# Two weight loads of the expert layers wait until the routed rows are in memory

## The chip, the cores and the metric

The kernel runs on one core of one Trainium2 chip. Its time is the device time of one execution in microseconds (us). The engines of the core run side by side and meet at semaphores: TensorE (PE) multiplies, VectorE (DVE) and ScalarE (ACT) do element work, GpSimd (POOL) issues the indirect transfers here, and SyncE (SP) only issues DMA transfers, in the order of its program. ACT issues transfers too, on a DMA queue of its own. All queues of the core share the same 16 DMA engines.

## The reference

Two blocks of two layers each work on 512 tokens of width 1024, in float32. The first block holds both places that the change touches: after its forgetting attention (layer 0) and after its retention (layer 1) comes a mixture of 32 experts. A router picks two experts for each token, and each expert is a gated product:

```
hn = rms_norm(h, norm_ffn[i])
gi = top-1 group of softmax(hn @ wr_g + br_g)            # 4 groups of 8 experts
e1, e2 = top-2 experts inside the group, by hn @ wr_e + br_e
gates = p_group * p_expert / sum(p_expert)
# for every expert e, on the tokens that chose it:
a, b = split(x @ w_gu[e])                                 # w_gu[e]: 1024 x 1024
y = (silu(a) * b) @ w_down[e]                             # w_down[e]: 512 x 1024
h = h + sum of gates * y
```

The second block (window attention, latent attention, neighbourhood attention) follows and isn't touched.

## The kernel before, in words

A list of stages is run by each engine in order. `run` (L2238) makes every engine wait, at the start of a stage, until the other engines have finished the stage before it, with a few exceptions; SP isn't held by that and runs ahead as far as the semaphores of its own loads let it.

Stage `RouteProj` (tags `fo1` in layer 0, `ro3` in layer 1) is the last part of the mixer's output projection together with the router. PE fills eight PSUM banks (L907), DVE adds them to the residual rows `H` (L1044), PE turns the rows and makes router logits (L870, L880), and DVE chooses the experts and works out to which row of the DRAM buffer `xg_dram` each token goes (L1033). This is done for two halves of 256 tokens. After each half POOL scatters the token rows with four indirect transfers of 128 rows of 4 KB (L859), one per token tile and choice. At the end of its stage POOL waits until all eight have landed (semaphore `route_scattered`). DVE meanwhile works out the overflow lists (to L1108).

Stage `Experts` (`ex0`, `ex1`) starts when all engines have finished `RouteProj`. ACT first issues two loads of 512 KB, each of 128 rows of `xg_dram` for two experts (L1314), on its own queue. PE turns the first block (L1203), DVE scales it (L1273), and then for every expert PE multiplies by the two halves of `w_gu` (L1210), turns the hidden rows (L1216), and multiplies by `w_down` of the expert before (L1222); ACT stores each expert's result with two transfers of 128 KB (L1287).

The weights are 96 loads of 2 MB, numbered v = 0 to 95, three for each expert (v = 3e and 3e+1 are the halves of `w_gu`, v = 3e+2 is `w_down`). They go into eight slots, v modulo 8: slots 0 to 2 lie in `ring`, slots 3 to 7 in `arena`. `Experts.sp` (L1169) issues the first eight in the order 0, 1, 3, 4, 5, 6, 2, 7. Loads 2 and 7 come last, since their slots are set free last: 2 needs the ring slot that holds the projection's weights, and waits for the last bank to be filled (`outproj_filled`); 7 in layer 0 waits for the same, since its slot overlaps what the projection reads, and in layer 1 for an earlier stage, but stands behind 2 in SP's program. Load 8 reuses slot 0 and waits until PE has used it (`experts_gated`), load 9 waits for `experts_upped`, load 10 for `experts_downed`, each of the first expert, and so on.

When the experts are done, stage `Combine` gathers the results with indirect transfers (L1387) and adds them to `H`.

Of the kernel before, what the change touches and what calls it, by code (L numbers as in the profile page):

```python
# [25 lines left out]
NT, NCT = SEQ // P, CTX // P  # L26
# [72 lines left out]
def build(nc, io):  # L99
    ctx = ExitStack()  # L100
    with ctx:
# [82 lines left out]
        class Weights:  # L184
# [20 lines left out]
            @classmethod  # L205
            def load(cls, sp, u):
                if u >= RING:
                    sp.wait_ge(*cls.freed[u - RING])
                for at, k, n, src in cls.units[u]:
                    sp.dma_start(cls.view(u, at, k, n), src.rearrange("(k p) n -> p k n", p=P))\  # L210
                        .then_inc(w_ready[u % RING], 16)
# [5 lines left out]
        class Stage:  # L217
# [25 lines left out]
            def sp(self, sp): pass  # L243


        class Start(Stage):
# [49 lines left out]
            def sp(self, sp):  # L296
                sp.wait_ge(self.s("rows"), 16)
                sp.wait_ge(self.s("vec"), 11 * 16)
# [812 lines left out]
        class Experts(Stage):  # L1111
# [57 lines left out]

            def sp(self, sp):  # L1170
                for v in (0, 1, 3, 4, 5, 6, 2, 7, *range(self.SLOTS, 3 * NE)):
                    e, what = divmod(v, 3)
                    if v < RING:
                        sp.wait_ge(*Weights.freed[self.base + v - RING])
                    elif v < self.SLOTS:
                        k = self.after(v - RING)
                        if k is None:
                            sp.wait_ge(*self.route.after_last)
                        else:
                            for other in done:  # L1180
                                sp.wait_ge(done[other], k + 1)
                    else:
                        sp.wait_ge(*self.used(v - self.SLOTS))
                    src = self.dn[e] if what == 2 else self.gu[e, :, 4 * what:4 * what + 4, :]
                    sp.dma_start(self.weights(v), src).then_inc(self.s(f"ready{v % self.SLOTS}"), 16)

                sp.wait_ge(self.s("open"), self.at("open") + 1)
                n = sp.value_load(ovn[0:1, 0:1], min_val=0, max_val=EXTRA)
                with sp.If(n > 0):
                    for j in range(EXTRA):  # L1190
                        with sp.If(n > j):
                            if j == 0:
                                sp.wait_ge(self.s("downed"), self.at("downed") + NE)
                            e = sp.value_load(ovn[0:1, 1 + j:2 + j], min_val=0, max_val=NE - 1)
                            for half in range(2):
                                sp.dma_start(self.weights(half), self.gu[e, :, 4 * half:4 * half + 4, :]).then_inc(self.s("x_weights"), 16)
                            sp.dma_start(self.weights(2), self.dn[e]).then_inc(self.s("x_weights"), 16)
                            sp.wait_ge(self.s("x_down"), j + 1)
# [1078 lines left out]
```

## Time and profile before

| | us |
|---|---|
| median of 3 runs (lowest, highest) | 3311.79 (3311.49, 3312.02) |
| the profiled execution | 3320.4 |
| its span in the trace | 3318.3 |
| PE busy | 2850.2 (86%) |
| DVE busy | 845.4 (25%) |
| ACT busy | 646.1 (19%) |
| POOL busy | 192.5 (6%) |

The profile page divides the span into 40 slices of 83 us. The line of DMA throughput stands at 427 to 428 GB/s in slices 8 to 11 and 21 to 25: these are the two expert stages. The page's chain of work that ended last is short here and names only the last norm, so what bounds a stage is read from the timeline, the windows and the waits. Times in the timeline are counted from the start of the span.

### The profile page before, as it was taken

Reading aid. Unit: us, or ns where it says so; the run is one execution under the profiler, and the core shown is the slowest. Engines: PE = TensorE matmul, PEld = TensorE weight load, DVE = VectorE, ACT = ScalarE, POOL = GpSimd, SP = SyncE. Lnnn points to the kernel's source line nnn. Section 1 sums busy time; section 2 is a strip of 40 time slices with the busy share of each in tenths; the row PEclk is TensorE's granted clock in tenths of the full one; section 3 lists DMA queues with packets and bytes.
Section 4 is the critical chain, followed back from the end, with each engine's and each line's share of the span. In section 5 each row is a group of like instructions: output and inputs, shape, how many; then the busy total and the mean of one; then the engine's idle time right before and its main releaser. Section 6 shows DMA issues by size and latency. Waiting matters only on the chain. (4 is left out here: it accounts for less than half of the span.)

```text
span 3318.3 us, 30730 instructions
## 1 busy us (share of the span) xinstructions
PE 2850.2 (86%) x12370; PEld 1418.1 (43%) x12370; DVE 845.4 (25%) x2217; ACT 646.1 (19%) x1394; POOL 192.5 (6%) x144
## 2 busy tenths in 40 slices
PE   7999868887758999998788778489999997999997
PEld 3454533222224444444322222156656563555554
DVE  1130331111112202112201101314624443054054
ACT  2120410000001000101100000213513342152143
POOL 1000000000000000000000000200010102012001
PEclk9999979999998999999899999799999998999999
DMA  5602249999984332225799999510010011121100
GB/s 186 235 26 76 102 177 396 427 427 428 427 326 162 113 126 102 102 76 205 294 428 427 427 427 427 221 41 19 1 39 27 28 37 54 52 66 48 51 23 32
DMA packets 117647, 604.84 MB, mean 182 GB/s; under 512 B 9701, under 2 KB 23978, under 8 KB 92794
## 3 DMA queue, kind: packets, MB, share of 16 engines
q1 hardware_dynamic: 91632, 537.15, 40.0%
q10 hardware_dynamic: 20618, 46.89, 4.0%
q0 software_dynamic: 5248, 18.75, 1.6%
q8 instruction: 102, 1.67, 0.2%
q14 instruction: 47, 0.39, 0.0%
HBM read 559.17 MB, written 43.52 MB: 182 GB/s over the span
## 5 line engine op out<-in xcount | busy, mean ns | idle before, releaser
L480 PE MATMUL psum<-ring,XT 128*128 128x512 f32 (+3 forms) x1216 | 480.1, 555 | 14.8 <-ACT arena L1863 6.6
L470 PE MATMUL psum<-XT,ring 128*128 128x512 f32 (+1 forms) x1152 | 444.2, 547 | 2.8 <-DVEq L2236 2.8
L1210 PE MATMUL psum<-arena,XT 128*64 128x512 f32 x1280 | 311.1, 633 | 105.6 <-DMA arena<-in_expert_w_gu 105.4
L480 PEld LDWEIGHTS psum<-ring,XT 128*128 128x128 f32 x1216 | 230.2, 190 | 256.3 <-issue 222.4
L470 PEld LDWEIGHTS psum<-XT,ring 128*128 128x128 f32 x1152 | 219.3, 191 | 226.8 <-issue 215.6
L562 PE MATMUL psum<-ring,arena 128*128 128x512 f32 x576 | 250.7, 593 | 6.8 <-DVEq L2236 4.3
L1210 PE MATMUL psum<-ring,XT 128*64 128x512 f32 x768 | 192.4, 649 | 71.8 <-DMA ring<-in_expert_w_gu 68.9
L687 PE MATMUL psum<-arena 64*128 64x384 f32 (+8 forms) x704 | 224.0, 505 | 27.4 <-ACT arena L741 22.3
L1280 DVE TENSOR_TENSOR XT<-XT,psum 64x512 f32<-64x512 f32 x64 | 44.1, 690 | 691.7 <-ACT XT L1283 691.7
L1210 PEld LDWEIGHTS psum<-arena,XT 128*64 128x64 f32 x1280 | 92.6, 144 | 295.9 <-issue 176.2
L1283 ACT ACTIVATE XT<-psum 64x512 f32<-64x512 f32 x64 | 37.7, 589 | 691.5 <-PE psum L1210 691.5
L562 PEld LDWEIGHTS psum<-ring,arena 128*128 128x128 f32 x576 | 108.1, 190 | 140.1 <-issue 129.6
L741 ACT ACTIVATE arena<-psum,rt 128x768 f32<-128x768 f32 (+5 forms) x224 | 158.2, 706 | 38.9 <-DVE rt L2143 20.4
L729 ACT ACTIVATE arena<-psum 128x512 f32<-128x512 f32 (+3 forms) x336 | 145.0, 467 | 98.1 <-PE psum L705 96.6
L705 PE MATMUL psum<-cst,arena 128*128 128x128 f32 x944 | 148.9, 284 | 12.5 <-DVE arena L785 6.7
L1222 PE MATMUL psum<-arena,XT 128*64 128x512 f32 x640 | 144.9, 595 | 1.1 <-DVE XT L1277 1.1
L755 DVE TENSOR_REDUCE rt<-psum 128x1 f32<-128x256 f32 (+5 forms) x160 | 99.6, 623 | 168.2 <-PE psum L689 100.3
L508 ACT ACTIVATE arena<-psum 128x512 f32<-128x512 f32 x64 | 36.5, 570 | 531.2 <-PE psum L480 366.2
L705 PEld LDWEIGHTS psum<-cst,arena 128*128 128x128 f32 x944 | 111.0, 144 | 66.1 <-issue 33.9
L1210 PEld LDWEIGHTS psum<-ring,XT 128*64 128x64 f32 x768 | 58.3, 147 | 189.2 <-issue 120.2
L687 PEld LDWEIGHTS psum<-arena 64*128 64x128 f32 (+3 forms) x704 | 97.1, 197 | 83.5 <-ACT arena L741 34.7
L716 PE MATMUL psum<-arena 128*64 128x128 f32 x1888 | 128.5, 280 | 4.7 <-ACT arena L729 4.7
(273 smaller groups left out, 2400.6 us busy)
## 6 DMA issues: line engine op xcount, KB each, us to landing
arena<-in_expert_w_gu SPq DMA_DIRECT2D x80, 2048.0 KB, 24.6
ring<-in_expert_w_gu SPq DMA_DIRECT2D x48, 2048.0 KB, 24.6
arena<-in_expert_w_down SPq DMA_DIRECT2D x40, 2048.0 KB, 28.2
ring<-in_expert_w_down SPq DMA_DIRECT2D x24, 2048.0 KB, 28.1
ring<-in_ada_w SPq DMA_DIRECT2D x12, 2048.0 KB, 8.9
ring<-in_fox_w_in SPq DMA_DIRECT2D x8, 2048.0 KB, 8.5
XT<-xg_dram ACTq DMA_DIRECT2D x32, 512.0 KB, 10.2
y_dram<-XT ACTq DMA_DIRECT2D x128, 128.0 KB, 8.8
```

What stands on the lines that cost most here:

```text
L470: i = pe.matmul(ps[0][0:cols_[1] - cols_[0], 0:ntok], w[:, c, cols_[0]:cols_[1]], x[:, c, tok:tok + ntok], start=(c == 0), stop=(c == k - 1))
L480: i = pe.matmul(ps[0][:, 0:width], x[:, c, t * P:(t + 1) * P], w[:, c, c0:c0 + width], start=(c == 0), stop=(c == k - 1))
L562: i = pe.matmul(bank(self.bank0 + n % 4), self.x[:, c, t * P:(t + 1) * P], w[:, c, half * BANK:(half + 1) * BANK], start=(c == 0), stop=(c ...
L687: ins = pe.matmul(self.s_at(n, c0, c1), lhsT, rhs, start=True, stop=True)
L705: i = pe.transpose(bank(b)[:, j * P:(j + 1) * P], self.P[:, u % 4, (k0 + j) * P:(k0 + j + 1) * P], ident)
L716: ins = pe.matmul(psum[hh * DH:(hh + 1) * DH, (6 + pair % 2) * BANK + i * P:(6 + pair % 2) * BANK + (i + 1) * P], v(h + hh, kt), self.PT[: ...
L729: act.activation(self.PT[:, m % 2, u % 2, k0:k0 + k, :], bank(b)[:, 0:k * P].rearrange("p (k q) -> p k q", k=k), ACT.Copy)\
L741: act.activation(self.P[:, n % 4, 0:hi - lo], self.s_at(n, lo, hi), ACT.Exp, bias=sm[:, 0, n:n + 1], accum_out=sm[:, 1, n:n + 1]).then_inc ...
L755: ins = dve.tensor_reduce(sm[:, 0, n:n + 1], self.s_at(n, *self.window(n)), AXX, ALU.max, negate=True)
L1210: i = pe.matmul(psum[side * BR:(side + 1) * BR, 0:FF], x[:, 4 * part + c, :], w[:, c, side * FF:(side + 1) * FF], start=(part == 0 and c = ...
L1222: i = pe.matmul(psum[half * BR:(half + 1) * BR, 5 * BANK:6 * BANK], self.HT[:, c, :], w[:, c, half * BANK:(half + 1) * BANK], start=(c == ...
L1280: return dve.tensor_tensor(self.HR[0:BR], self.SA, psum[P - BR:P, 0:FF], ALU.mult)
```

## The change

Before SP comes to load 2, it now also waits until all eight scatters of this layer have landed (16 counts for each of the 2 x 4 transfers). Load 7 stands behind it in SP's program and so waits too.

```
             def sp(self, sp):
                 for v in (0, 1, 3, 4, 5, 6, 2, 7, *range(self.SLOTS, 3 * NE)):
+                    if v == 2:
+                        sp.wait_ge(*self.route.n("scattered", 16 * 2 * NT))
                     e, what = divmod(v, 3)
                     if v < RING:
                         sp.wait_ge(*Weights.freed[self.base + v - RING])
```

No instruction changes its place on any engine. SP's program at the start of the expert stage of layer 0, before the change (each row is a transfer with what it waits for; x2 stands for two such):

```order
L1185 DMA ring<-in_expert_w_gu 128x4096 [waits products_filled] x2
L1185 DMA arena<-in_expert_w_gu 128x4096 [waits done_dve,done_pool,done_act,done_pe] x2
L1185 DMA arena<-in_expert_w_down 128x4096 [waits done_dve,done_pool,done_act,done_pe]
L1185 DMA arena<-in_expert_w_gu 128x4096 [waits done_dve,done_pool,done_act,done_pe]
L1185 DMA ring<-in_expert_w_down 128x4096 [waits outproj_filled]
L1185 DMA arena<-in_expert_w_gu 128x4096 [waits outproj_filled]
L1185 DMA ring<-in_expert_w_down 128x4096 [waits experts_gated]
```

And after it (the lines of the file stand two further down):

```order
L1187 DMA arena<-in_expert_w_gu 128x4096 [waits done_dve,done_pool,done_act,done_pe] x2
L1187 DMA arena<-in_expert_w_down 128x4096 [waits done_dve,done_pool,done_act,done_pe]
L1187 DMA arena<-in_expert_w_gu 128x4096 [waits done_dve,done_pool,done_act,done_pe]
L1187 DMA ring<-in_expert_w_down 128x4096 [waits outproj_filled,route_scattered]
L1187 DMA arena<-in_expert_w_gu 128x4096 [waits outproj_filled]
L1187 DMA ring<-in_expert_w_down 128x4096 [waits experts_gated]
```

Load 2 (the first `w_down` into `ring`) has the new wait; load 7 follows it. In layer 1 the same row has the same second wait.

## Rows read from the trace of the kernel before

**Rows 1.** The page's costliest groups: PE's products by the first expert weights.
```profile
L1210 PE MATMUL psum<-arena,XT 128*64 128x512 f32 x1280 | 311.1, 633 | 105.6 <-DMA arena<-in_expert_w_gu 105.4
L1210 PE MATMUL psum<-ring,XT 128*64 128x512 f32 x768 | 192.4, 649 | 71.8 <-DMA ring<-in_expert_w_gu 68.9
```

**Rows 2.** Windows, layer 0: PE, PEld, DVE, ACT, POOL, clock, DMA share, GB/s.
```profile
465.00:474.00 9.00, 0.48 (x3) 0.34 (x2) 8.14 (x36) 1.34 (x9) 3.79 (x4) 0.50 0.99 386
474.00:477.00 3.00, 0.00 (x0) 0.00 (x0) 0.16 (x1) 0.00 (x0) 0.53 (x1) 0.50 0.04 16
481.00:489.00 8.00, 6.58 (x19) 1.96 (x19) 1.23 (x1) 0.00 (x0) 0.00 (x0) 0.55 0.01 2
502.00:507.00 5.00, 5.00 (x28) 2.35 (x27) 1.91 (x2) 0.92 (x2) 0.00 (x0) 1.00 0.30 105
509.00:970.00 461.00, 370.32 (x1665) 132.07 (x1662) 50.16 (x73) 35.22 (x60) 0.00 (x0) 0.97 1.00 423
```

**Rows 3.** Timeline of SP, layer 0: start, length, engine, line, transfer, count.
```profile
453.37 0.33 SPq L1185 DMA_DIRECT2D ring<-in_expert_w_down  x1
453.74 0.43 SPq L1185 DMA_DIRECT2D arena<-in_expert_w_gu  x1
489.26 0.33 SPq L1185 DMA_DIRECT2D ring<-in_expert_w_down  x1
492.70 14.18 SPq L1185 DMA_DIRECT2D ring<-in_expert_w_gu  x2
506.92 0.43 SPq L1185 DMA_DIRECT2D arena<-in_expert_w_down  x1
```

**Rows 4.** Timeline of POOL, DVE, ACT and PE at layer 0's hand-over.
```profile
469.60 0.95 POOL L859 DMA_INDIRECT xg_dram<-arena,top8i  x1 [0.30 <-issue]
474.00 0.16 DVE L1108 TENSOR_TENSOR gates<-gates,rt 128x4 f32<-128x4 f32 x1
476.18 0.84 ACTq L1314 DMA_DIRECT2D XT<-xg_dram  x2
479.59 1.95 PE L1203 MATMUL psum<-cst,XT 128*128 128x128 f32 x8 [14.11 <-DMA XT<-xg_dram]
482.95 9.70 PE L1210 MATMUL psum<-ring,XT 128*64 128x512 f32 x32 [1.42 <-DVE XT L1273]
```

**Rows 5.** Timeline of the same engines and SP, layer 1.
```profile
1580.21 0.33 SPq L1185 DMA_DIRECT2D ring<-in_expert_w_down  x1
...
1596.84 0.95 POOL L859 DMA_INDIRECT xg_dram<-arena,top8i  x1 [0.30 <-issue]
...
1601.24 0.16 DVE L1108 TENSOR_TENSOR gates<-gates,rt 128x4 f32<-128x4 f32 x1
1604.30 0.81 ACTq L1314 DMA_DIRECT2D XT<-xg_dram  x2
...
1611.00 8.88 PE L1210 MATMUL psum<-ring,XT 128*64 128x512 f32 x32 [1.42 <-DVE XT L1273]
```

**Rows 6.** Windows, layer 1, the columns of rows 2.
```profile
1602.00:1604.20 2.20, 0.00 (x0) 0.00 (x0) 0.00 (x0) 0.00 (x0) 0.00 (x0) 0.50 0.02 9
1609.00:1616.00 7.00, 5.58 (x19) 1.84 (x19) 1.22 (x1) 0.00 (x0) 0.00 (x0) 0.60 0.00 0
1637.00:2100.00 463.00, 378.56 (x1672) 135.03 (x1670) 50.58 (x74) 35.58 (x60) 0.00 (x0) 0.96 0.99 421
```

**Rows 7.** L1314: the first row load at 476.18; the 13 from 525.4 to 903.9.
```profile
DMA to landing us min/median/max: 3.3/3.3/3.3
...
DMA to landing us min/median/max: 10.0/10.2/10.9
```

**Rows 8.** L1287: the store issued at 970.4; the store issued at 507.2.
```profile
DMA to landing us min/median/max: 2.2/2.2/2.2
...
DMA to landing us min/median/max: 7.3/7.3/7.3
```

**Rows 9.** L1387: the 16 indirect gathers of `Combine`, both layers.
```profile
DMA to landing us min/median/max: 4.2/5.7/6.5
```

More of the change, by code:

```diff
@@ L1171, in sp @@
                 for v in (0, 1, 3, 4, 5, 6, 2, 7, *range(self.SLOTS, 3 * NE)):
+                    if v == 2:
+                        sp.wait_ge(*self.route.n("scattered", 16 * 2 * NT))
                     e, what = divmod(v, 3)
```

## The prediction

> **What bounds the kernel now.** I began with the page's costliest groups. PE's products by the first expert weights have 105.6 + 71.8 us of idle time in front of them, ended almost only by weight loads [rows 1]. The windows of the expert stage of layer 0 say why: from 509 to 970 us the DMA engines are busy all the time and move 423 GB/s, and PE works 370 of 461 us [rows 2]; in layer 1 it is 421 GB/s from 1637 to 2100 [rows 6]. So the body of the stage lasts as long as its 2 MB loads take, and one load is 2097 KB / 423 GB/s = 4.96 us.
>
> The question is then when that unbroken stream starts. SP's timeline [rows 3] shows load 8 at 489.26 and load 9 at 492.70, the second transfer of that row (load 10) just before 506.9, then loads 11 and 12. Between them the DMA engines are all but idle: share 0.01 from 481 to 489, 0.30 from 502 to 507 [rows 2]; in layer 1 0.00 from 1609 to 1616 [rows 6]. These loads wait for slots, which means for PE's first expert. So the start of the stream is set by PE's first products, and these are set by a chain that the timeline shows link by link [rows 4]: the last scatter is issued at 469.60; ACT issues the row loads at 476.18; the first block has landed when PE turns it at 479.59; products start at 482.95. A delay of that chain moves the stream and its end by as much, since nothing behind it has slack; a gain likewise.
>
> **What the change does, part by part.** It moves 4 MB for each layer. Before, loads 2 and 7 are issued at 453.37 and 453.74 [rows 3], at 1580.21 in layer 1 [rows 5], beside the scatters. Afterwards they are issued when the last scatter lands, which is also the event that lets POOL end its stage and ACT issue the row loads.
>
> Cost at nothing: the wait itself (SP has nothing else to do), and load 8 behind it. That one isn't due before about 489 + 6; from a release near 475.5, loads 2 and 7 with the two row blocks are 5 MB, 5.24 / 0.423 = 12.4 us, over near 488. PE needs load 2 for its first product by `w_down`, behind the 32 + 32 products of two experts: some 20 us after 482.95 (the store after it is issued at 507.2). Load 7 is for the third expert, later still. The cover for both is the time of PE's first two experts; were it gone, each missing load would cost up to 4.96 us.
>
> Term A, a gain: the scatters of the second half no longer share. From 465 to 474 the DMA engines are full (share 0.99), and from 474 to 477 empty (0.04) [rows 2]. The last scatter goes out at 469.60, ACT's row load at 476.18, 6.6 us later; in layer 1 it is 1596.84 to 1604.30, 7.5 us. What an undisturbed indirect transfer takes isn't seen for a scatter. The nearest row is the gather of the same size with an idle machine: 5.7 us [rows 9]. That gives 0.9 and 1.8 us, together 2.7, which I take. Bounds: nothing at all, if the last scatter's landing is slow for a reason of its own; and at most 2.0 + 2.9 = 4.9, since DVE ends its stage only at 474.16 and 1601.40 [rows 4, 5], and ACT waits for that too.
>
> Term B, a cost: the first row block shares the DMA engines with loads 2 and 7. Alone, it lands 3.3 us after its issue [rows 7]. With the weight stream beside it, 13 such loads took 10.0 to 10.9, median 10.2: 6.9 us more [rows 7]. But two stores of 128 KB were often ahead of these on the same queue, which the first block won't have. A case with nothing ahead on ACT's queue is the first store at 507.2: weight loads had been issued within the microsecond before, at 506.92 and just ahead of it [rows 3], as they will be here, and it landed after 7.3 us against 2.2 for one alone [rows 8], 5.1 us more, with a quarter of the bytes. So the block pays between 5.1 and 6.9; I take the middle, 6.0, for each layer, 12.0 together. As bounds I keep nothing (the row block is served first) and 7.6 (the longest of the 13, 10.9 against 3.3) for each layer. The block lands at about 475.3 + 9.3 = 484.6, well inside the 12.4 us that the four transfers keep the engines busy, so it is never released from sharing early.
>
> The Trainium skill ("DMA: Bandwidth & Descriptors", "Queues, rings and completion order") says that a DMA engine goes round the queues that have work by whole packets, not by single descriptors. By it the row block would wait for one whole weight load, if that reached the engines first, and for nothing if it came first. The store's 5.1 us [rows 8] agrees with one load; the 6.9 of the row blocks [rows 7] is more than that. By this rule the sum would be +7.2 us (first rival) in place of the one below.
>
> Term C, of either sign: TensorE's clock. At the hand-over the granted clock is 0.50 (1.2 GHz) [rows 2], PE having been idle for 14.11 us [rows 4], and it rises to 2.4 GHz during the first products, earlier in layer 1 than in layer 0: the 32 products took 9.70 and 8.88 us [rows 4, 5]. Where it rises may move, 0.8 us for each layer, 1.6 together; I take zero.
>
> Sum: 12.0 - 2.7 = +9.3 us. The profiled execution took 3320.4 for a span of 3318.3; it lies 8.6 above the median of the runs, so I add the difference to the median: 3311.8 + 9.3 = 3321.1 us, 0.28% slower. Its own range, from the nearer bounds: 2 x 5.1 - 4.9 - 1.6 = +3.7 to 2 x 7.6 + 1.6 = +16.8.
>
> **Rivals.**
>
> *One load's wait per layer.* Each DMA engine finishes its share of load 2 before it turns to the row block, and then serves that at once: 2 x 4.96 - 2.7 = +7.2, 3319.0. (The Trainium skill's rule above would make it so.) For it: the store. Against it: the row blocks, and that the second of a pair of stores isn't a further load behind the first.
>
> *The row block isn't slowed; not slower.* Place: ACT's queue at 475.5 and 1602.5. SP and ACT are released by the same landing, a few tenths of a microsecond apart. If the row block's share of each DMA engine is taken up before load 2's, it lands in 3.3 as now, and only term A is left: -2.7, 3309.1, which is within 0.2%. With term A at its bound, -4.9. It decides if the landing of the first block stays below 3.3 + 1.4 us (2.7 / 2). For it: the block alone needs little more than a microsecond of the engines. Against it: SP waits for the semaphore directly, while ACT waits behind POOL's end of stage, and the late store of [rows 8], issued just behind weight loads, was not let through.
>
> *First come, first served.* Both weight loads go ahead of the row block: 2 x 2 x 4.96 - 2.7 = +17.1, 3328.9. For it: SP issues load 7 only 0.37 us behind load 2 [rows 3], so both may be in front. Against it: the row blocks of [rows 7] never waited over 10.9, with several loads outstanding.
>
> *The shift is absorbed,* because the stream has room: the time stays within 3 us of before. For it: the stream is short of work only by PE's 370 of 461 us. Against it: that is PE's slack, not the DMA engines' (share 1.00 from 509 on [rows 2]), and it is they that set the end.
>
> **Chances and numbers.** My forecast 0.62; one load's wait 0.15; the block not slowed 0.10; first come 0.05; absorbed 0.08. About 0.2%, 6.6 us, is what a measurement of this kernel can tell from no change. The forecast lies above that in about 0.8 of its cases (0.50), one load's wait in 0.6 (0.09), first come always (0.05), together 0.64; I add 0.02 for costs that I haven't named. Faster by 0.2% would need 6.6 us, more than term A can give; 0.03 for clock and chance. The rest, 0.31, is no change. Range: leaving out the block not slowed and most of first come, and the ends of my own, 3313 to 3327.
>
> **What would show it.** In the profile after: loads 2 and 7 at the same time as ACT's row loads, near 475.5 and 1602.5 (term A; if they stay at 476.2 and 1604.3, term A was nothing). The first row load of each layer landing after 8.4 to 10.2 us instead of 3.3 (term B), and PE's first turn (L1205 there) at about 484.7 instead of 479.59. DMA share near 1 from 477 to 489, where it is near 0 now from 481. The windows of the body as long as before, 461 and 463 us at the same GB/s, only later: 5.1 us in layer 0 (6.0 - 0.9), 9.3 in all by the end of layer 1. I'm wrong if the first block lands within 5 us, or if PE's first turn is late but the stage's last product isn't.

## The result and the profile after

| | before | changed |
|---|---|---|
| median of 6 runs (us) | 3311.9 | 3324.99 |
| lowest to highest | 3310.8 to 3316.31 | 3324.59 to 3326.81 |
| ratio, 95% interval | | 1.0032 (1.0022 to 1.0043) |

The kernel became 13.1 us slower by the medians, +0.32% by the ratio (0.22 to 0.43%). The forecast was +9.3 us. In all later comparisons the kernel before had medians of 3312.8 to 3313.7 us and single runs from 3308 to 3320; so total times decide little below 3 us here, and I read each cause from the traces.

The timeline of the changed kernel at layer 0's hand-over: start, length, engine, line, transfer or operation. It answers to [rows 3] and [rows 4].

```profile
469.07 0.95 POOL L859 DMA_INDIRECT xg_dram<-arena,top8i  x1 [0.30 <-issue]
...
473.18 0.33 SPq L1187 DMA_DIRECT2D ring<-in_expert_w_down  x1
...
473.48 0.16 DVE L1108 TENSOR_TENSOR gates<-gates,rt 128x4 f32<-128x4 f32 x1
473.55 0.43 SPq L1187 DMA_DIRECT2D arena<-in_expert_w_gu  x1
474.33 0.94 ACTq L1316 DMA_DIRECT2D XT<-xg_dram  x2
...
485.96 1.94 PE L1205 MATMUL psum<-cst,XT 128*128 128x128 f32 x8 [21.02 <-DMA XT<-xg_dram]
...
489.32 8.48 PE L1212 MATMUL psum<-ring,XT 128*64 128x512 f32 x32 [1.42 <-DVE XT L1275]
494.41 0.33 SPq L1187 DMA_DIRECT2D ring<-in_expert_w_down  x1
```

Read it from the last scatter on. ACT's row loads go out 5.26 us later, against 6.58 before: the undisturbed scatters gain 1.3. SP has issued load 2 1.15 us ahead of them and load 7 0.78 ahead. PE's first turn comes 11.63 us behind the row loads, against 3.41 before: this is the loss. In layer 1 the same holds, as the same view shows ([rows 5] before; the first line here is the turn before, 3.34 us behind the row loads):

```profile
1607.64 1.94 PE L1203 MATMUL psum<-cst,XT 128*128 128x128 f32 x8 [14.92 <-DMA XT<-xg_dram]
```

```profile
1601.01 0.95 POOL L859 DMA_INDIRECT xg_dram<-arena,top8i  x1 [0.30 <-issue]
1605.21 0.33 SPq L1187 DMA_DIRECT2D ring<-in_expert_w_down  x1
...
1606.37 0.92 ACTq L1316 DMA_DIRECT2D XT<-xg_dram  x2
...
1617.13 1.94 PE L1205 MATMUL psum<-cst,XT 128*128 128x128 f32 x8 [20.27 <-DMA XT<-xg_dram]
...
1620.50 9.49 PE L1212 MATMUL psum<-ring,XT 128*64 128x512 f32 x32 [1.42 <-DVE XT L1275]
```

The landing of the first row load of each layer, where [rows 7] has 3.3:

```profile
DMA to landing us min/median/max: 11.5/11.5/11.5
...
DMA to landing us min/median/max: 10.6/10.6/10.6
```

The windows say whether the body of the stage changed (length, busy time of PE, PEld, DVE, ACT, POOL, granted clock, DMA share, GB/s), as in [rows 2] and [rows 6]:

```profile
475.00:488.00 13.00, 1.94 (x8) 1.57 (x8) 0.00 (x0) 1.28 (x1) 0.01 (x1) 0.50 0.93 387
488.00:494.00 6.00, 4.68 (x16) 1.57 (x18) 1.23 (x1) 0.00 (x0) 0.00 (x0) 0.65 0.02 4
507.00:512.00 5.00, 5.00 (x27) 2.35 (x28) 1.92 (x2) 0.89 (x2) 0.00 (x0) 1.00 0.30 105
515.00:975.00 460.00, 374.76 (x1660) 133.17 (x1657) 50.16 (x73) 35.21 (x60) 0.00 (x0) 0.96 1.00 423
1645.00:2110.00 465.00, 372.24 (x1682) 133.51 (x1680) 50.58 (x74) 35.63 (x60) 0.00 (x0) 0.97 0.99 420
```

The moved 4 MB fill the DMA engines from 475 to 488, where PE waits for the 512 KB that go with them; then the engines stand idle until PE's first expert sets slots free (0.02, and 0.30 from 507 to 512, as before). The body runs at 423 and 420 GB/s, against 423 and 421 before.

The best measure of the stage is the time from the last scatter to the first gather of `Combine`, since it leaves out what the other 2300 us of the execution do. These are the gathers, of layers 0 and 1 before and of layers 0 and 1 in the changed kernel:

```profile
981.68 0.99 POOL L1387 DMA_INDIRECT arena<-y_dram,didx  x1 [504.83 <-ACTq L2236]
...
2107.75 0.99 POOL L1387 DMA_INDIRECT arena<-y_dram,didx  x1 [502.78 <-ACTq L2236]
```

```profile
986.79 0.99 POOL L1389 DMA_INDIRECT arena<-y_dram,didx  x1 [511.79 <-ACTq L2238]
...
2117.80 0.99 POOL L1389 DMA_INDIRECT arena<-y_dram,didx  x1 [510.76 <-ACTq L2238]
```

986.79 - 469.07 = 517.72 and 2117.80 - 1601.01 = 516.79, together 1034.5. Before, with the last scatters at 469.60 and 1596.84, it was 512.08 and 510.91, together 1023.0. So the two stages took 11.5 us more. The profiled execution of the changed kernel took 3325.33, near its median, while that of before (3320.4) lay 8.6 above its own. Outside the two stages it took 6.3 us more than that of the changed kernel, 4.9 of them behind the last gather (2107.75 to 3318.3 is 1210.6 us, 2117.80 to 3323.5 is 1205.7), in code that is the same. So the spans differ by 11.5 - 6.3 = 5.2 us, while the medians differ by 13.1.

Below, "sum" is this time over both layers, "landing" the time from issue to landing of each layer's first row load, and its "delay" what the landing takes beyond the 3.3 and 3.2 us of before. A "piece" is one record of what a DMA engine moved: the trace has them with queue, start, length and size, and they show 16 KB for a weight load and 4 KB for a row load.

### The profile page after: what moved, and what is told of

It reads as the page before. It is cut to its first block and busy times, and to the rows that moved or that the text cites. A ratio compares the mean times of both kernels' runs of the same rounds, so it can differ in the third digit from the quotient of the medians.

```text
span 3323.5 us, 30732 instructions
## 1 busy us (share of the span) xinstructions
PE 2841.8 (86%) x12370; PEld 1414.8 (43%) x12370; DVE 843.6 (25%) x2217; ACT 647.0 (19%) x1394; POOL 193.2 (6%) x144
## 5 line engine op out<-in xcount | busy, mean ns | idle before, releaser
L741 ACT ACTIVATE arena<-psum,rt 128x768 f32<-128x768 f32 (+5 forms) x224 | 158.4, 707 | 34.7 <-DVE rt L2145 17.5
```

The source lines that it names most:

```text
L741: act.activation(self.P[:, n % 4, 0:hi - lo], self.s_at(n, lo, hi), ACT.Exp, bias=sm[:, 0, n:n + 1], accum_out=sm[:, 1, n:n + 1]).then_inc ...
```

## The experiments

**Loads after the rows.** SP waits for the row blocks instead of the scatters:

```
                     if v == 2:
-                        sp.wait_ge(*self.route.n("scattered", 16 * 2 * NT))
+                        for a in range(2):
+                            sp.wait_ge(self.s(f"rows{a}"), self.at(f"rows{a}") + 16)
```

> Loads 2 and 7 wait until both row blocks have landed, not only the scatters. My theory (the loss is the first row block sharing the DMA engines with the two loads, the gain is that the scatters don't share): the row block lands 3.3 us after its issue as in the kernel before, the gain of 1.3 and 2.1 us stays, so about 3.4 us faster than before: 3308.5 us. Rival (the loads come too late for the first expert, or the stream starts later for another reason): still slower than before, 3320 us or more, with the row block landing early and PE waiting for load 2.

Landing 3.1 and 3.2 us; sum 1019.95, 3.0 less than before and 14.6 less than the changed kernel. Total 3310.92 against 3313.67, ratio 0.9993 (0.9984 to 1.0003), which alone doesn't tell it from no change. Load 2 goes out at 480.87, 9.8 us behind the last scatter against 4.1 in the changed kernel, and nothing waits for it:

```profile
471.04 0.95 POOL L859 DMA_INDIRECT xg_dram<-arena,top8i  x1 [0.30 <-issue]
...
476.28 0.84 ACTq L1317 DMA_DIRECT2D XT<-xg_dram  x2
...
479.55 1.95 PE L1206 MATMUL psum<-cst,XT 128*128 128x128 f32 x8 [12.64 <-DMA XT<-xg_dram]
480.87 0.33 SPq L1188 DMA_DIRECT2D ring<-in_expert_w_down  x1
...
482.92 9.28 PE L1213 MATMUL psum<-ring,XT 128*64 128x512 f32 x32 [1.42 <-DVE XT L1276]
```

So lateness of the two loads costs nothing, and their company with the first row block costs the whole loss. The gain on the scatters stands here alone: the row loads follow the last scatter after 5.24 us as in the changed kernel.

**One load beside the rows.**

```
-                    if v == 2:
+                    if v == 7:
                         sp.wait_ge(*self.route.n("scattered", 16 * 2 * NT))
```

> Only load 7 waits for the scatters, load 2 goes at the old place: one load beside the row block instead of two. By turns (the queues are served alternately): the row block can be held up by all of the one load at most, 4.96 us; I expect 4 to 5 us more than alone, landing 8 us after its issue, and some of the gain on the scatters lost, total +6 us, 3318. First come, first served: also 4.96. If the row block's delay were independent of how much weight data is in flight (a fixed price of sharing), it would stay at about 11 us, total near +12.

Landing 7.7 and 7.3, 4.4 and 4.1 more than alone; sum 1028.9, +5.9; total 3318.32, ratio 1.0017 (1.0007 to 1.0026). With only 2 MB in flight the delay stays below one load's 4.96 us. It isn't one fixed price of sharing. The gain on the scatters was whole here too (5.27 and 5.38 us to the row loads), not partly lost as I had expected.

**Three loads beside the rows.** The same line with `v == 6`.

> Loads 6, 2 and 7 wait: three loads beside the row block. Served by turns: the row block's landing stays where it is with two loads, 10.8 to 11.6 us after its issue, so the total is that of the changed kernel, 3325 us, within 2. First come, first served: each further load puts 4.96 us on each layer, landing at 15 to 16.5 us, total 3335 us.

Landing 10.8 and 10.7; sum 1035.3, against 1034.5 with two loads; total 3325.97, ratio 1.004 (1.0026 to 1.0054). A third load ahead of the row block adds nothing (10.8 and 10.7 against 11.5 and 10.6). First come, first served is out: it would put one more load's 4.96 us on each layer. The queues are served in turns, and the block's delay is bounded.

**Smaller pieces.** Loads 2 and 7 as two transfers of 512 columns each (the count that PE waits for goes up by 16 in these slots):

```
-                    sp.dma_start(self.weights(v), src).then_inc(...)
+                    for part in ((slice(0, 512), slice(512, 1024)) if v in (2, 7) else (slice(0, 1024),)):
+                        sp.dma_start(self.weights(v)[:, :, part], src[:, :, part]).then_inc(...)
```

> As the changed kernel, but loads 2 and 7 are each issued as two transfers over 512 of the 1024 columns, so that they are made of pieces of 2 KB instead of 16 KB; bytes the same. If the DMA engines alternate between the queues piece by piece, the row block (eight pieces of 4 KB for each engine) is held up eight times by 2 KB instead of 16 KB: its landing falls from about 11 us to 4.5 to 6 us, total 3313 to 3316 us. If they serve by bytes or by whole transfers, or first come first served, the landing stays at 9 to 12 us, total 3321 to 3327 us.

Landing 7.3 and 7.0: delays of 4.0 and 3.8 instead of 8.2 and 7.4, with the same bytes. Sum 1027.6; total 3318.7, ratio 1.0016 (1.0006 to 1.0026). My figure was too low: not all of the delay goes with the size of a piece. And the order of issue isn't quite the same, since SP takes 1.31 us for the two transfers of load 2, so that load 7 comes behind the row loads:

```profile
470.07 1.31 SPq L1188 DMA_DIRECT2D ring<-in_expert_w_down  x2
...
471.22 0.90 ACTq L1317 DMA_DIRECT2D XT<-xg_dram  x2
...
471.43 1.35 SPq L1188 DMA_DIRECT2D arena<-in_expert_w_gu  x2
```

Fewer bytes issued ahead of the block would shorten its delay too. What decides between the two is below, in the pieces.

**A control that wasn't one.** The same two transfers, split by partitions (0 to 63 and 64 to 127), with pieces of 16 KB.

> Control for the run with 2 KB pieces, which also had twice as many transfers: loads 2 and 7 are each issued as two transfers over 64 partitions, pieces stay 16 KB. If the size of a piece decides, the first row block lands after 10.5 to 11.5 us as with whole loads. If the number or size of the transfers decides (turns by transfer), it lands at 7 to 7.5 us as in that run.

Landing 17.9 and 17.5, sum 1048.9, total 3339.91 in two runs: neither of the two outcomes. The windows show why:

```profile
476.00:488.00 12.00, 0.00 (x0) 0.00 (x0) 0.00 (x0) 0.00 (x0) 0.00 (x0) 0.50 1.00 227
```

Transfers over 64 partitions kept the DMA engines busy all the time and moved 227 GB/s, where whole loads move 423. The delays, 14.6 and 14.3, are nearly twice those of the changed kernel (7.4 to 8.2). That fits a fixed number of weight pieces ahead of the block, each taking about twice as long (median 1.1 us, where those of a whole load take 0.61), but the run changed the rate together with the split, and its times can't decide between turns by piece and by transfer.

**Pieces of 8 KB.** Two transfers again, split in the middle dimension: `self.weights(v)[:, part]` with `slice(0, 2)` and `slice(2, 4)`.

> Loads 2 and 7 as two transfers each with pieces of 8 KB. Turns by piece: eight pieces of 8 KB ahead of the row block's cost 2.5 us against 4.9 (16 KB) and 0.6 (2 KB), so landing between the two, 8.6 to 9.2 us. Turns by transfer: 7 to 7.5, as with 2 KB pieces.

Landing 9.2 and 8.5, sum 1029.8, total 3320.88, ratio 1.0017 (1.0007 to 1.0028). This is the better control: the same number and size of transfers as with 2 KB pieces, and 1.5 to 1.9 us later. It speaks against turns by whole transfer, though load 7's first half was issued 0.31 us ahead of the row loads here, and behind them with 2 KB pieces. The three sizes lie on a line: mean delay 3.9 us for 2 KB, 5.6 for 8 KB, 7.8 for 16 KB. From 2 to 16 KB it rises by 3.9; eight pieces on each engine (128 rows over 16 engines), 14 KB bigger, at 423/16 = 26.4 GB/s are 8 x 14.3 / 26.4 = 4.3 us. What is left at size nothing is about 3.3 us. The line mixes two things, though, since with smaller pieces less of load 7 is ahead of the row loads; the pieces below separate them.

**Rows asked for first.** ACT counts a semaphore when it has issued both row loads, and SP waits for that:

```
                     if v == 2:
-                        sp.wait_ge(*self.route.n("scattered", 16 * 2 * NT))
+                        sp.wait_ge(self.s("asked"), self.at("asked") + 1)
...
                 rows(1)
+                act.nop().then_inc(self.s("asked"), 1)
```

> SP's loads 2 and 7 wait only until ACT has issued its two row loads (not until these have landed), so the row blocks have a head start of under a microsecond instead of a handicap of 1.15 us. Turns by piece with a head start: the first block needs only 1.3 us of the engines, most of it is through before weight data flow, landing 3.3 to 5.5 us after its issue. If sharing has a fixed price whoever comes first: 9 to 11 us. The time between last scatter and gather, summed over both layers, 1020 to 1024 us by the first (before 1023.0, changed 1034.5), 1030 to 1034 by the second.

```profile
474.14 0.84 ACTq L1316 DMA_DIRECT2D XT<-xg_dram  x2
475.05 0.33 SPq L1187 DMA_DIRECT2D ring<-in_expert_w_down  x1
475.42 0.43 SPq L1187 DMA_DIRECT2D arena<-in_expert_w_gu  x1
477.60 1.95 PE L1205 MATMUL psum<-cst,XT 128*128 128x128 f32 x8 [12.85 <-DMA XT<-xg_dram]
```

Landing 3.3 and 3.3, no delay at all, with load 2 issued 0.91 us behind the row load; sum 1019.6; total 3312.51, ratio 0.9996 (0.9986 to 1.0006). Two microseconds of order of issue, from 1.15 ahead to 0.91 behind, are the difference between 8 us and nothing. The pieces show the mirror image: load 2's first piece starts 3.0 us behind its issue, when nearly all 256 pieces of the two row blocks have started.

**Released together.** SP waits for the end of POOL's stage, which is what releases ACT:

```
-                        sp.wait_ge(*self.route.n("scattered", 16 * 2 * NT))
+                        sp.wait_ge(done["pool"], timeline.index(self.route) + 1)
```

> SP's loads 2 and 7 wait for the end of POOL's stage, the same event that releases ACT, so the loads' head start over the row block falls from 1.15 us to 0.2 or less. Delays so far over a block alone: 3.4 us plus eight pieces (16 KB: 8.2 and 7.4, 8 KB: 5.9 and 5.3, 2 KB: 4.0 and 3.8) with the loads 1.15 us ahead, 0 with them 0.9 us behind. Turns by piece, with the 3.4 us made of the head start and about 2.2 us of weight pieces already taken up: 7 us less 0 to 1, landing 9 to 10.5 us after its issue. If the order of arrival decides alone, and the two now arrive together: anything from 3.3 to 11 us, and not the same in the two layers.

```profile
472.15 0.33 SPq L1187 DMA_DIRECT2D ring<-in_expert_w_down  x1
472.23 0.84 ACTq L1316 DMA_DIRECT2D XT<-xg_dram  x2
```

Landing 9.5 and 9.3, delays of 6.2 and 6.1, alike in both layers. With the head start gone, 2.0 and 1.3 us of the delay go, and some 4.9 + 1.2 stay: eight pieces of 16 KB and a little. SP, released by POOL's end of stage, issues 0.08 us ahead of ACT in both layers, so it is this that ACT waits for. In the changed kernel SP saw the scatters landed 4.1 us after the last one's issue; POOL's end of stage adds the 1.15. The sum was 1030.2, +7.2. The total's three runs (3323.1 to 3331.31, ratio 1.0043, 1.0028 to 1.0058) are higher than this sum explains; what the unprofiled ones did can't be seen.

**What the pieces show.** For the first row block, layers 0 and 1: when its first piece starts after the issue, how long it takes from there to the last of its 16 completion records (one for each DMA engine), and how many weight pieces start in that time beside how many row pieces (those beyond 128 are of the second block).

| | first piece (us) | from there (us) | weight pieces / row pieces |
|---|---|---|---|
| before | 1.0, 1.0 | 1.9, 1.9 | none |
| changed kernel | 3.9, 3.8 | 7.2, 6.4 | 149 / 148, 136 / 135 |
| one load | 3.7, 3.7 | 3.5, 3.3 | 40 / 178, 41 / 154 |
| three loads | 3.7, 3.6 | 6.7, 6.6 | 140 / 142, 138 / 140 |
| 2 KB pieces | 3.5, 3.2 | 3.4, 3.5 | 290 / 189, 315 / 192 |
| 8 KB pieces | 3.7, 3.8 | 5.0, 4.3 | 174 / 161, 154 / 142 |
| released together | 2.8, 2.7 | 6.2, 6.2 | 127 / 134, 128 / 128 |
| rows asked first | 1.1, 1.0 | 1.9, 2.0 | none |

The second column is the taking of turns. With whole loads one weight piece goes for each row piece, 0.61 us for 16 KB and then 0.16 us for 4 KB, back and forth on each engine. With 8 KB it is still nearly one for one, each 0.31 us; with 2 KB it is about three for two, each 0.08. With one load in flight the weight pieces run out. So it is the size of the pieces that shortened the delay with 2 KB: in layer 0 the second column fell by 3.8 us and the first, where the order of issue would show, by 0.4. The first column is the other part of the delay: the queue that comes second waits 1.7 to 2.9 us longer for its first piece than alone, with little regard to the size of the pieces (2.5 and 2.2 with 2 KB) or the number of loads (2.7 with three). Why it waits so long no run shows.

**Layer 0 only.** `if v == 2 and self.l == 0:`

> The new wait in layer 0 only. The cost is local to each layer: last scatter to first gather 517 to 518.5 us in layer 0 and 510.5 to 511.5 in layer 1 (before 512.1 and 510.9), total half of the change's, +5.6, 3317 us. Rival (something couples the layers, or the rest of the measured 13 us is elsewhere): a sum away from +5 to +7.

Last scatter to gather 517.51 in layer 0 (with the wait) and 510.40 in layer 1 (without), sum +4.9; total 3317.99, ratio 1.0015 (1.0005 to 1.0025). The cost is local and the two layers add up.

**Rows first again, with more rounds.**

> The same kernel as the first with rows first, beside the warm one, with more rounds: its sum of last scatter to gather was 1019.95 against 1023.0, so 3 us faster than before, ratio 0.999; the first comparison couldn't tell it from no change. Rival: the gain on the scatters isn't in the total time at all, ratio 1.000.

Sum 1019.7, 3.3 less than before; total 3313.33 against 3313.08, ratio 0.9998 (0.9989 to 1.0007). The two traces agree within 0.3 us on a gain of 3 us, and the totals can't show it: the interval is three times as wide.

**Rows first, with TensorE kept at work.** At the end of `RouteProj.pe` and before the first turn:

```
                 self.ranks(pe, 1)
+                for _ in range(9):
+                    pe.matmul(bank(self.free(0)), ident, cst[:, 0:BANK], start=True, stop=True)
...
                 pe.wait_ge(self.s("padded"), self.at("padded") + 1)
+                for _ in range(5):
+                    pe.matmul(bank(7), ident, cst[:, 0:BANK], start=True, stop=True)
                 turn(0)
```

> Rows first (loads 2 and 7 after both row blocks have landed), and TensorE is kept at work between its last product of the router and the first row block: 9 products of 512 columns before the end of its stage and 5 after, into a bank that nobody reads. If the first expert's slow products are the clock's doing, they take 7.1 us as at full clock instead of 9.3 and 9.7, the turns 1.2 instead of 1.9: about 3 us for each layer less than rows first alone, 6 together; last scatter to gather 507 in each layer, sum 1014 (before 1023.0). If the added products delay the stage's end or the clock doesn't rise in time, the sum stays at 1020 or more.

The timeline of PE in layer 0:

```profile
465.69 10.78 PE L920 MATMUL psum<-cst 128*128 128x512 f32 x18
477.23 4.53 PE L1248 MATMUL psum<-cst 128*128 128x512 f32 x10 [0.76 <-POOL XT L1359]
481.59 1.05 PE L1208 MATMUL psum<-cst,XT 128*128 128x128 f32 x8
484.07 7.09 PE L1215 MATMUL psum<-ring,XT 128*64 128x512 f32 x32 [1.42 <-DVE XT L1280]
```

The first expert's products took 7.09 us in both layers, against 8.5 to 9.9 in all the runs above, and the granted clock was 1.00 (2.4 GHz) in them, where the kernel before had 0.50 (1.2 GHz) from 483 to 488: the slow first expert is the clock. But the added products ended late (each shows as two, 18 took 10.78 us), so the row loads went out 6.5 and 6.1 us after the last scatter instead of 5.3. Sum 1017.8; total 3309.26 against 3313.08, ratio 0.9983 (0.9974 to 0.9992).

**Fewer added products,** 5 and 3.

> As the warm kernel, with 5 added products before the stage's end instead of 9, and 3 after it instead of 5. In the warm kernel the first expert ran at full clock (7.09 us), but the added products ended late: the row loads went out 0.8 to 1.3 us and the turn began 2.5 to 3 us later than with rows first alone. If 5 and 3 fit into the wait and the clock still rises before the turn: row loads 5.3 us after the last scatter, turn 8.6 to 8.8, products 7.1 long, sum of last scatter to gather 1013 to 1015, 8 to 10 us less than before's 1023.0, ratio about 0.9975. If the clock doesn't rise in time: products 8 us or longer and the sum 1017 or more.

```profile
464.45 6.21 PE L920 MATMUL psum<-cst 128*128 128x512 f32 x10
474.84 4.41 PE L1248 MATMUL psum<-cst 128*128 128x512 f32 x6 [4.18 <-POOL XT L1359]
479.09 1.05 PE L1208 MATMUL psum<-cst,XT 128*128 128x128 f32 x8
481.56 7.09 PE L1215 MATMUL psum<-ring,XT 128*64 128x512 f32 x32 [1.42 <-DVE XT L1280]
```

Row loads 5.25 and 5.37 us after the last scatter and products of 7.09 us, as hoped; but PE then had a gap of 4.18 us, the records of the three further products took 4.41 us (granted clock 0.62 from 475 to 479), and the turn behind them began 10.3 us after the last scatter where the block had landed at 8.5. The sum was 1017.8, not the 1013 to 1015 that I had expected. Total 3306.04 against 3312.81, ratio 0.998 (0.9971 to 0.9989): the fastest version here, and the interval keeps it below the kernel before. Of its 6.8 us the sums give 3.2 to rows first and 2.0 to the added products; 1.6 stay unexplained.

## Why the prediction was right, and what it got wrong

What bounds the stage: right. The first gather is 5.6 and 5.9 us further from the last scatter, and PE's first product by `w_down` 5.7 and 5.9 (38.93 and 39.18 us against 33.25 and 33.24): the delay at the start arrives whole at the end, and nothing absorbed it.

Term A, the gain on the scatters, taken as 2.7: it was 1.3 + 2.1 = 3.4. The row loads follow the last scatter after 5.24 to 5.38 us in every trace in which load 7 waits, also where load 2 went early, but for the run with nine added products. The gathers' landing [rows 9] came near this by luck: the last scatter landed after 4.1 us, and POOL's end of stage made up the rest. How the loads got in the way I had wrong too. The pieces before the change show loads 2 and 7 of layer 0 wholly moved at 468.6, 1 us before the last scatter was issued. They shared with the scatters of the first half, whose last piece started at 469.0 instead of 458.2 in the changed kernel; the second half, issued from 465.84 on, stood behind these.

Term B, the row block's company, taken as 12.0: this is the term that was mis-sized. From row load to first turn it was 11.63 and 10.76 us against 3.41 and 3.34, together 15.6, above the 15.2 of its bounds. The row that I leaned on, a store at 507.2 that landed 5.1 us late, has four pieces for each engine; a row block has eight, and waits in its turn eight times. The upper row, 6.9 for the blocks in the body, was nearer, though below both; I had reasoned that the blocks in the body had stores ahead of them and the first one wouldn't, and took the middle. What I left out was load 2's head start of 1.15 us: the run with both released together landed at 9.5 and 9.3 us. That this is just the 9.3 that I forecast is in part luck, since the 6.0 in it was the middle between two rows and no count of pieces.

Term C, the clock, taken as zero: -1.2 and +0.6 (8.48 and 9.49 us for the first products against 9.70 and 8.88), together -0.6. The sum is within the 1.6 allowed, layer 0 alone beyond its 0.8.

Together: 15.6 - 3.4 - 0.6 = 11.6 against 11.5 by the sums. The medians' 13.1 leaves 1.5 us that these terms don't explain; the ratio's interval (7 to 14 us) holds both. The direction, the path and the mechanism of term B were right, that of term A in part; the size came out as near as it did because A and C gave 1.3 us more back than I had counted, against the 3.6 that B cost more.

The rivals. First come, first served is refuted by the run with three loads and by the pieces; it would have given 17.1 for the change. The block not slowed, not slower: its condition (block first) was not met, since SP is released 1.15 us ahead of ACT, but its mechanism is real and was shown when SP was made to wait 0.91 us longer than ACT. I had written that the two were released "a few tenths" apart; POOL's end of stage is what lies between them. One load's wait: the delay with a single load in flight, 4.4 and 4.1, fits it in number only, since the row pieces went in between that load's own, and that with two, 8.2 and 7.4, doesn't fit. The Trainium skill's rule ("DMA: Bandwidth & Descriptors", "Queues, rings and completion order"), that turns go by packets of some 9 to 17 descriptors, isn't what these runs show if one whole load is one packet: the delay grew past one load's 4.96 us, and 149 weight pieces went beside 148 row pieces, one by one. Absorbed: refuted.

What stays open: the part of the delay that doesn't depend on the size of a piece, 3.3 us by the line. Most of it is the wait for the first row piece, 2.2 to 2.9 us longer than alone with the head start and 1.7 to 1.8 without. In the changed kernel 1376 and 1296 KB of weights started before that piece. Whether the engines had taken them up already, no run shows.

## What to carry to other kernels

When a transfer on the critical path is released by the same event as bulk transfers, the order of issue decides: let the small one be asked for first, and make the bulk wait for that (or for its landing), if its consumers leave room, as here some 20 us. A wait that keeps bulk transfers away from one critical step must also be checked against the next: here it took 4 MB off the scatters, worth 3.4 us, and put them onto the row load, worth 15.6. Where the order can't be changed, smaller pieces in the bulk stream shorten the turns: +4.6 us by the sums with 2 KB instead of +11.5. And where a stage is bound by a stream of loads, look at what its first slots wait for, since every microsecond there is paid in full at the end.

## What the runs showed of the hardware that I hadn't expected

- Two queues with work on the same DMA engines were served in turns of one piece, 16 KB of weights (0.61 us) and 4 KB of rows (0.16 us), 149 beside 148; the delay of a 512 KB load of 4 KB pieces rose with the size of the stream's pieces (3.9, 5.6 and 7.8 us for 2, 8 and 16 KB) and not with the number of loads beyond two (7.5 us with three).
- The queue that came second waited for its first turn: 1.7 to 1.8 us longer than alone when it was issued 0.08 us behind, 2.8 to 2.9 us when 1.15 us behind.
- A head start of 0.91 us was enough for the 512 KB load to land as if alone, in 3.3 us.
- Loads of 1 MB over 64 partitions moved 227 GB/s with the DMA engines busy all the time, against 423 for loads over 128.
- TensorE's granted clock was 0.50 (1.2 GHz) after its idle time at the hand-over, and the first 32 products took 8.5 to 9.9 us; with products put into the wait it had come back to 1.00 (2.4 GHz), and they took 7.09.
